# Bidirectional GLA encoder trunk: one rounded product per tile for the decay gate logits

## The chip, the cores and the metric

The kernel runs on one core of a Trainium2 chip. The metric is the device time of one execution in microseconds; a shorter one is better. The engines are PE (TensorE matrix products), DVE (VectorE), ACT (ScalarE), POOL (GpSimd) and SP, which here only issues transfers.

## The reference, cut to what matters

One encoder layer over 2560 tokens (512 and 2048) of width 1024. A projection of the normed input feeds gated linear attention (GLA) in both directions, differential attention and attention into a memory; they are gated, merged and projected. The change is about the decay gates of the GLA:

```python
glr = glr.astype(jnp.float32).reshape(B, T, 2, GLA_RANK)          # 2 x 16 columns of the projection
gate_logits = jnp.einsum('btir,irk->btik', glr, w2.astype(jnp.float32)) + b2.astype(jnp.float32)
log_a = jax.nn.log_sigmoid(gate_logits) / GLA_TAU
...
b = jnp.cumsum(ac, axis=2)                                        # per chunk, inside gla_scan
```

## The kernel before, in words

The kernel is a row of phases: projection (names `proj_`), forward GLA (`glaf_`), backward GLA (`glab_`), differential attention (`diff_`), cross attention (`cross_`) and merge (`merge_`). Each is a block with one hand-written instruction stream per engine; at its end all engines meet. A large product keeps the precision of fp32 by splitting both operands into a part rounded to fp32r and the rest, and adds three fp32r products (high x high, high x low, low x high).

**Projection.** Five chunks of 512 tokens, and the memory. In each chunk PE computes 8 "values" units, one "narrow" unit (the 32 gate columns) and 16 "stream" units of 24 products each. `product` gives the narrow unit 16 products: rows 0 to 31 of its bank take high x (high + low) and rows 32 to 63 take low x high, so the two halves are still to be added. ACT copies all 64 rows out of PSUM (`evacuate`, L393) and stores them to the scratch tensor `glrT`. DVE rounds the streamed weights (`split`, L476), one unit ahead where its order lets it, and POOL subtracts to get their low parts (L514); PE waits for that by `lo_split` before each stream unit.

**Forward GLA.** Twenty tiles of 128 tokens, all alike, each with 7 units of a second, independent product, `Dense` (168 fp32r products of 512 columns per tile), cut into slots between the GLA's own steps. Every unit of `Dense` needs a weight split: ACT rounds (L705), as soon as it has copied a finished unit out (L714), and POOL subtracts (L731, two inputs in SBUF). The tile's own chain is:

- PE: running sums of the log decays (L937), 60 dense products, `logits(j + 1)` (L920: one fp32 product of 65 rows, which the profile shows as two records), the plain scores (L951), 18 dense, level scores of the first group (L902, 56 records), 18 dense, level scores of the second group (L902, 48 records), and so on for the other direction, then outputs (L969 to L976) and 18 dense.
- ACT: exponents of the sums, then `softplus(j + 1)` on the new logits (L990 to L992), with the dense copies between.
- DVE: differences of the sums (L1091, L1092), four pairs of multiplications K and Q (`mix`, L1101 and L1103, two inputs in SBUF), between the third and the fourth pair the diagonal (L1128), after them `decays(j + 1)` (L1073, the rounding L1074, L1075), then the `copy_predicated` of the levels (L1139).

PE's second group of level scores may start when DVE has done the first four L1139 of the direction, since the four PSUM slots are used again:

```python
def levels(j, d, first, last):
    pe.wait_ge(picked_done, j * PK + 1 + d * NL + first)
```

The first tile is laid out a little differently in time, and the last one has no `logits` and no `decays`.

**Semaphores.** The two blocks made with `last=True` (differential attention and merge) end in a clearing of the semaphores used so far on POOL and one more barrier.

Of the kernel before, what the change touches and what calls it, by code (L numbers as in the profile page):

```python
# [12 lines left out]
P = 128  # L13
# [79 lines left out]
class Early:  # L93
# [113 lines left out]
def phase_project(nc, used, h, early, w_zg, w2, ident, x_all, gains, ident_dram, w_stream, w_narrow, w_values, w_mem, w_mem_values, hT_hi, hT_lo, featT, featT_lo, narrowT, values,  # L207
                  memkT, mem_v):

    with ExitStack() as ctx:  # L210
# [41 lines left out]
        stat = m.sb("stat", [P, 2, 4])  # L252
        acc = m.ps("acc", [P, BANKS, CH])
# [18 lines left out]
        low_stored = m.sems("low_stored", 2)  # L272
        stored = m.sems("stored", OUTS)
# [34 lines left out]
        @block.sync  # L308
        def _(sp):
            def load_x(n):  # L310
                if n >= 2:
                    sp.wait_ge(normed, n - 1)
                sp.dma_start(x[:, n % 2], rows(x_all, n * P, P)).then_inc(x_in[n % 2], 16)

            def load_piece(n):
                if n >= RAW:
                    sp.wait_ge(lo_split, n - RAW + 1)
                sp.dma_start(raw_of(n), source(n)).then_inc(raw_in[n % RAW], 16)

# [12 lines left out]
            for n in range(6, RESIDENT):  # L332
                load_piece(n)
            sp.dma_start(gain[:, 1], gains[:, 1]).then_inc(mem_gain_in, 16)
            for c in range(NC):
                for s in range(STREAM):
                    load_piece(RESIDENT + c * STREAM + s)
                    if s in (0, 1, 7, 8):
                        load_x((c + 1) * TT + (0, 1, 7, 8).index(s))
            for n in range(RESIDENT + NC * STREAM, len(pieces)):  # L340
                load_piece(n)
            sp.wait_ge(stored[narrow_units[0] % OUTS], 16 * (narrow_units[0] // OUTS + 1))
            early.load_gates(sp, narrowT, w2)
            sp.wait_ge(lo_split, len(pieces))
            early.load_w(sp, 0, w_zg, FORWARD_UNITS)

        @block.scalar
        def _(act):
# [32 lines left out]
            def evacuate(u):  # L381
                kind, c, i, t = units[u]
                act.wait_ge(unit_done, u + 1)
                if u >= OUTS:
                    act.wait_ge(stored[u % OUTS], 16 * (u // OUTS))
                    if in_parts(u - OUTS):
                        act.wait_ge(low_out, part_units.index(u - OUTS) + 1)
                if in_parts(u):
                    scale = HD ** -0.5 / SLOPES[i - DQ_BLOCK] if i < DK_BLOCK else 1.0
                    act.activation(out[:, u % OUTS].bitcast(FP32R), acc[:, u % BANKS], ACT.Copy, scale=scale).then_inc(evacuated, 1)  # L390
                else:
                    filled = slice(0, 2 * NR if kind == "narrow" else P)
# [12 lines left out]
                act.dma_start(dst, out[0:2 * NR if kind == "narrow" else P, u % OUTS]).then_inc(stored[u % OUTS], 16)  # L405
# [32 lines left out]
            for b in range(2):  # L438
                act.wait_ge(low_stored[b], 16 * (len(part_units) // 2))
            for b in range(OUTS):  # L440
                act.wait_ge(stored[b], 16 * ((len(units) + OUTS - 1 - b) // OUTS))

        @block.vector
        def _(dve):
# [41 lines left out]
            dve.memset(early.glr[4 * RANK:4 * RANK + 1, :, :], 1.0).then_inc(early.ones_ready, 1)  # L486
# [30 lines left out]
        def _(pe):  # L517
# [254 lines left out]
def phase_gla_forward(nc, used, h, early, ident, featT, narrowT, w2, v_dram, sums_dram, picked_dram, diag_dram,  # L772
                      o_dram, qb_dram, kb_dram, decb_dram, hT_hi, hT_lo, w_zg, zg):

    with ExitStack() as ctx:
# [8 lines left out]
        KR, N2 = 4 * RANK + 1, 2 * H * GK  # L784
# [6 lines left out]
        m.allocated += [*glr_in, decay_in, early.ones_ready]  # L791
# [68 lines left out]
        def _(sp):  # L860
# [33 lines left out]
        def _(pe):  # L894
# [28 lines left out]
            pe.wait_ge(decay_in, 16)  # L923
# [226 lines left out]
def phase_gla_backward(nc, used, h, early, ahead, ident, v_dram, o_dram, qb_dram, kb_dram, decb_dram, gain_dram, item_hi, item_lo, hT_hi, hT_lo, w_zg, zg):  # L1150

    with ExitStack() as ctx:
# [40 lines left out]
        block = m.block(used)  # L1193
# [190 lines left out]
def phase_diff(nc, used, ahead, front, ident, v_dram, lambda_dram, gain_dram, zg, item_hi, item_lo):  # L1384

    with ExitStack() as ctx:
# [72 lines left out]
        block = m.block(used, last=True)  # L1459
# [901 lines left out]
def build(nc, x_all, gains, w_stream, w_glr, w_values, w_mem, w_mem_values, w2, gla_sums, gla_picked, gla_diag,  # L2361
# [6 lines left out]
    featT, glrT = scratch("featT", N_FEAT, P, TOK), scratch("glrT", 4 * RANK, TOK)  # L2368
# [8 lines left out]
    with ExitStack() as ctx:  # L2377
# [3 lines left out]
        with ExitStack() as ahead_ctx:  # L2381
            with ExitStack() as gla_ctx:
# [3 lines left out]
                phase_project(nc, used, h, early, w_zg, w2, ident_tile, x_all, gains, ident, w_stream, w_glr, w_values, w_mem, w_mem_values, hT_hi, hT_lo,  # L2386
# [32 lines left out]
def layout(x_prompt, x_sample, mem_prompt, mem_sample, norm_g, w_in, gla_gate_w2, gla_gate_b, gla_norm_g,  # L2419
           diff_lambda, diff_norm_g, mem_norm_g, w_mem_kv, w_branch, w_out, final_norm_g):  # L2420
    w, at = w_in[0], OFFSETS
    w2 = np.zeros((4 * RANK + 1, 2, H * GK), w.dtype)
    for d in range(2):
        for part in range(2):
            w2[(2 * part + d) * RANK:(2 * part + d + 1) * RANK, d] = gla_gate_w2[0, d]
        w2[4 * RANK, d] = gla_gate_b[0, d]
# [12 lines left out]
        "w2": w2.reshape(4 * RANK + 1, -1),  # L2439
# [27 lines left out]
```

## Time and profile before

| | us |
|---|---|
| median of 3 runs | 3427.72 |
| lowest and highest run | 3424.59, 3429.3 |
| span of the profiled execution | 3421.6 |
| PE busy in the span | 3279.7 |
| forward GLA, PE from its first logits to the last level scores | 768.8 to 1746.4 |

The profiled execution is given by its span, from the first to the last instruction, 3421.6 us; the median of the timed runs is 6.1 us above it, which is what lies around the span. A row of a timeline has the start in us, the duration in us, engine, line, operation, output <- inputs, shape, how many instructions are merged, and in brackets how long the engine was idle before it and whose result ended that. A duration can hold time in which an issued instruction was still held up. Ends of PE rows are modelled, so what a PE instruction costs is read from start to start.

### The profile page before, as it was taken

To read this page: it belongs to the slowest core of one execution; us is meant where nothing else is said; L and a number is where in the kernel's file an instruction comes from. 1 tells how busy PE (TensorE), PEld (TensorE's weight loads), DVE (VectorE), ACT (ScalarE), POOL (GpSimd) and SP (SyncE) were. 2 spreads that over 40 slices of the span, in tenths; PEclk is the share of its full clock that TensorE was granted. 3 is DMA by queue.
4 is the path that set the end of the run, shared out by engine and by line. 5 is a ranking of instruction groups with operands and counts; after the bars stand their busy time and mean duration, and the time that the engine had idled before them with its cause. 6 is when DMAs were issued, how large, how long until landed. Compare 5 with 4: busy or idle time off the path is not lost. (4 is left out here: it accounts for less than half of the span.)

```text
span 3421.6 us, 51012 instructions
## 1 busy us (share of the span) xinstructions
PE 3279.7 (96%) x19032; PEld 2553.4 (75%) x19032; DVE 2014.6 (59%) x4689; ACT 1324.5 (39%) x2165; POOL 1223.2 (36%) x511
## 2 busy tenths in 40 slices
PE   7999999999999999999999988999999988999998
PEld 6888888877777777787777764666666556888887
DVE  3322312227556655665567788888888556556654
ACT  3111111114333433343333335666666555233332
POOL 3322313244333333333333326777777533000000
PEclk9999999999999999999999999999999999999999
DMA  6545445555454544544448964121221266666562
GB/s 213 182 156 184 167 153 167 179 200 182 137 176 136 184 146 129 183 145 137 130 160 288 324 215 139 59 75 55 73 65 38 99 218 234 222 234 231 181 216 77
DMA packets 317907, 554.90 MB, mean 162 GB/s; under 512 B 35421, under 2 KB 114525, under 8 KB 317662
## 3 DMA queue, kind: packets, MB, share of 16 engines
q1 hardware_dynamic: 266510, 471.26, 42.8%
q10 hardware_dynamic: 51152, 80.38, 6.5%
q8 instruction: 152, 2.49, 0.3%
q14 instruction: 93, 0.76, 0.1%
HBM read 382.03 MB, written 169.50 MB: 161 GB/s over the span
## 5 line engine op out<-in xcount | busy, mean ns | idle before, releaser
L731 POOL TENSOR_TENSOR glaf_w_lo<-early_raw,glaf_w_hi 128x1024 fp32r<-128x1024 f32 x140 | 350.7, 2506 | 650.3 <-ACT glaf_w_hi L705 650.3
L760 PE MATMUL glaf_dense_acc<-h_hi,glaf_w_hi 128*128 128x512 f32 x1120 | 452.7, 404 | 4.1 <-ACT glaf_dense_out L714 4.1
L760 PE MATMUL glaf_dense_acc<-h_lo,glaf_w_hi 128*128 128x512 f32 x1120 | 439.0, 392 | 0.0
L760 PE MATMUL glaf_dense_acc<-h_hi,glaf_w_lo 128*128 128x512 f32 x1120 | 436.8, 391 | 0.0
L1749 DVE CUSTOM_DVE_ANT_0 front_p<-diff_s_ps,ahead_table 128x512 f32<-128x512 f32 x544 | 346.7, 686 | 54.2 <-PE diff_s_ps L1611 53.0
L514 POOL TENSOR_TENSOR proj_w_lo<-early_raw,proj_w_hi 128x1024 fp32r<-128x1024 f32 x84 | 204.4, 2436 | 477.7 <-DVE proj_w_hi L476 477.7
L1572 POOL TENSOR_SCALAR front_p<-front_p,diff_ratio 128x1024 f32<-128x1024 f32 (+1 forms) x80 | 270.1, 3377 | 174.9 <-DVE diff_ratio L1769 174.9
L1692 ACT ACTIVATE front_p<-front_p,diff_neg_max 128x2048 f32<-128x2048 f32 (+1 forms) x160 | 278.9, 1744 | 10.1 <-DVE diff_neg_max L1759 10.0
L1635 PE MATMUL diff_oT_ps<-diff_aT,diff_v 128*128 128x512 f32 x544 | 273.8, 604 | 6.0 <-ACT diff_aT L1686 6.0
L201 PE MATMUL proj_acc<-h_hi,proj_w_hi 128*128 128x512 f32 x672 | 262.8, 391 | 0.0
L1610 PE MATMUL diff_s_ps<-ahead_k,ahead_q_high 128*128 128x512 f32 x544 | 245.1, 451 | 18.3 <-DVE diff_mx L1749 10.7
L203 PE MATMUL proj_acc<-h_hi,proj_w_lo 128*128 128x512 f32 x672 | 261.6, 389 | 0.0
L202 PE MATMUL proj_acc<-h_lo,proj_w_hi 128*128 128x512 f32 x672 | 261.5, 389 | 0.0
L760 PEld LDWEIGHTS glaf_dense_acc<-h_hi,glaf_w_hi 128*128 128x128 f32 x1120 | 211.8, 189 | 51.5 <-issue 7.9
L760 PEld LDWEIGHTS glaf_dense_acc<-h_hi,glaf_w_lo 128*128 128x128 f32 x1120 | 210.9, 188 | 45.6
L1139 DVE COPY_PREDICATED glaf_att<-glaf_picked,glaf_att_ps 128x256 f32<-128x256 int32 x280 | 146.7, 524 | 165.3 <-PE glaf_att_ps L902 158.4
L760 PEld LDWEIGHTS glaf_dense_acc<-h_lo,glaf_w_hi 128*128 128x128 f32 x1120 | 212.2, 189 | 40.6 <-issue 0.5
L1686 ACT ACTIVATE diff_aT<-diff_t_ps 128x512 f32<-128x512 f32 x272 | 159.4, 594 | 176.3 <-PE diff_t_ps L1624 176.2
L1624 PEld LDWEIGHTS diff_t_ps<-all_ident,diff_a 128*128 128x128 f32 x1088 | 133.9, 141 | 122.3 <-issue 95.4
L1611 PE MATMUL diff_s_ps<-ahead_k,ahead_q_low 128*128 128x512 f32 x544 | 217.2, 399 | 0.0
L393 ACT ACTIVATE proj_out<-proj_acc 128x512 f32<-128x512 f32 (+1 forms) x93 | 55.6, 598 | 412.0 <-PE proj_acc L203 394.5
L476 DVE CAST proj_w_hi<-early_raw 128x1024 fp32r<-128x1024 f32 x84 | 59.6, 715 | 251.8 <-PE proj_acc L203 251.8
(216 smaller groups left out, 7167.6 us busy)
## 6 DMA issues: line engine op xcount, KB each, us to landing
early_raw<-in_w_zg SPq DMA_DIRECT2D x180, 512.0 KB, 4.8
early_raw<-in_w_stream SPq DMA_DIRECT2D x80, 512.0 KB, 3.7
scratch_zg<-glaf_dense_out SPq DMA_DIRECT2D x140, 256.0 KB, 2.3
items_raw<-in_w_br SPq DMA_DIRECT2D x120, 256.0 KB, 2.9
merge_gate<-scratch_zg SPq DMA_DIRECT2D x120, 256.0 KB, 3.1
scratch_featT<-proj_out ACTq DMA_DIRECT2D x80, 256.0 KB, 2.3
items_br_hi<-scratch_item_hi SPq DMA_DIRECT2D x60, 256.0 KB, 5.9
items_br_lo<-scratch_item_lo SPq DMA_DIRECT2D x60, 256.0 KB, 6.4
```

What stands on the lines that cost most here:

```text
L201: pe.matmul(out, a_hi, b_hi, start=first, stop=False)
L202: pe.matmul(out, a_hi, b_lo, start=False, stop=False)
L203: return pe.matmul(out, a_lo, b_hi, start=False, stop=last)
L514: pool.tensor_tensor(lo, raw_of(n), hi, ALU.subtract).then_inc(lo_split, 1)
L731: pool.tensor_tensor(self.w_lo[:, s], self.raw[:, u % self.RAW], self.w_hi[:, s], ALU.subtract).then_inc(self.lo_split, 1)
L760: done = pe.matmul(self.acc[:, u % self.banks], a, x, start=i == 0, stop=i == self.PER - 1)
L1572: pool.tensor_scalar(p[:, o.slot, 1, half], p[:, o.slot, 1, half], ratio[:, o.slot:o.slot + 1], None, ALU.mult).then_inc(far_scaled, 1)
L1610: pe.matmul(s_ps[:, chunk % 2, i], q_high[:, b, i, cols], k[:, key % KS, i], start=True, stop=False)
L1611: done = pe.matmul(s_ps[:, chunk % 2, i], q_low[:, b, i, cols], k[:, key % KS, i], start=False, stop=True)
L1635: pe.matmul(oT_ps[:, :], v[:, o.head % 2, kt], aT[:, unit % 2], start=kt == 0, stop=kt == o.nk - 1).then_inc(values_done, 1)
L1692: act.activation(p[:, o.slot, i, 0:o.T], p[:, o.slot, i, 0:o.T], ACT.Exp, bias=neg_max[:, o.slot, i:i + 1], scale=SLOPES[o.h], accum_out=s ...
L1749: dve.tensor_tensor_reduce(out=p[:, n.slot, i, c * KC:(c + 1) * KC], in0=s_ps[:, (n.c0 + c) % 2, i], in1=table[:, start:start + KC], scale ...
```

## The change

The logits come from one fp32r product of 98 rows. For that the 32 gate rows are made whole in the projection (the two halves added) and split into a rounded and a low part: ACT copies rows 32 to 63, DVE adds them to rows 0 to 31 in PSUM, ACT rounds the sum out, DVE subtracts to get the low part. `glrT` now holds rounded, rounded again, low (96 rows), by three stores of 32 rows instead of one of 64, and two rows of ones stand below. The weight `decay_w` is split in the same manner by four DVE instructions (`split_decay`) ahead of chunk 1, from a load that SP issues early in the projection. Semaphores are cleared behind the backward GLA and no longer behind the differential attention.

```diff
-        self.glr = m.sb("glr", [4 * RANK + 1, 2, P])
-        self.decay_w = m.sb("decay_w", [4 * RANK + 1, 2 * H * GK])
+        self.glr = m.sb("glr", [GATE_ROWS, 2, P], FP32R)
+        self.decay_w = m.sb("decay_w", [GATE_ROWS, 2 * H * GK], FP32R)
...
+    def split_decay(self, dve, raw, pick):
+        whole = self.decay_w[:, :].bitcast(FP32)
+        step = Chain(dve, self.decay_steps)
+        dve.wait_ge(self.decay_in, 32)
+        step(dve.tensor_copy(self.decay_w[:, :], raw))
+        step(dve.tensor_tensor(raw, raw, whole, ALU.subtract))
+        step(dve.tensor_scalar(raw, raw, pick[:, 1:2], None, ALU.mult))
+        step(dve.scalar_tensor_tensor(self.decay_w[:, :], whole, pick[:, 0:1], raw, ALU.mult, ALU.add))
...
+            early.load_decay(sp, decay_raw[:, :], decay_pick[:, :], w2, w2_pick)
...
+                elif kind == "narrow":
+                    act.activation(out[0:NR, u % OUTS], acc[NR:2 * NR, u % BANKS], ACT.Copy).then_inc(gate_steps, 1)
+                    act.wait_ge(gate_steps, 3 * c + 2)
+                    act.activation(out[0:NR, u % OUTS].bitcast(FP32R), acc[0:NR, u % BANKS], ACT.Copy).then_inc(evacuated, 1)
...
                 if kind == "narrow":
-                    dst = narrowT[:, cols]
...
+                    act.dma_start(narrowT[0:NR, cols], out[0:NR, u % OUTS]).then_inc(gate_stored, 16)
+                    act.dma_start(narrowT[NR:2 * NR, cols], out[0:NR, u % OUTS]).then_inc(gate_stored, 16)
+                    act.wait_ge(gate_steps, 3 * c + 3)
+                    act.dma_start(narrowT[2 * NR:3 * NR, cols], out[NR:2 * NR, u % OUTS]).then_inc(stored[u % OUTS], 16)
+                    return
...
+            def gate_parts(u):
+                c, s = units[u][1], u % OUTS
+                near = acc[0:NR, u % BANKS]
+                dve.wait_ge(gate_steps, 3 * c + 1)
+                dve.tensor_tensor(near, near, out[0:NR, s], ALU.add).then_inc(gate_steps, 1)
+                dve.wait_ge(evacuated, u + 1)
+                dve.tensor_tensor(out[NR:2 * NR, s], near, out[0:NR, s], ALU.subtract).then_inc(gate_steps, 1)
...
             for u, (kind, c, i, t) in enumerate(units):
                 at = u - first_unit[c]
+                if u - 1 in narrow_units:
+                    gate_parts(u - 1)
+                if u == first_unit[1]:
+                    early.split_decay(dve, decay_raw[:, :], decay_pick[:, :])
                 for n in split_at.get(u, ()):
                     split(n)
...
+                    if u - BANKS in narrow_units:
+                        pe.wait_ge(gate_steps, 3 * units[u - BANKS][1] + 3)
...
-            pe.wait_ge(decay_in, 16)
+            pe.wait_ge(early.decay_steps, 4)
```

In each chunk the two new DVE instructions stand between two weight roundings. DVE before, in chunk 1 behind the narrow unit's start (L476 rounds the weights of stream units 0 and 1; `h_lo` belongs to the next chunk's norm):

```order
173 L458 SCALAR_TENSOR_TENSOR proj_xn<-proj_x,proj_stat,proj_gain 128x1024 [waits proj_transposed,proj_steps]
174 L476 CAST proj_w_hi<-early_raw 128x1024 [waits proj_unit_done,proj_raw_in1]
175 L476 CAST proj_w_hi<-early_raw 128x1024 [waits proj_unit_done,proj_raw_in2]
176 L465 TENSOR_TENSOR h_lo<-proj_tp,h_hi 128x4x128 [waits proj_hi_ready]
177 L465 TENSOR_TENSOR h_lo<-proj_tp,h_hi 128x4x128
```

The same place on DVE in the changed kernel:

```order
179 L487 SCALAR_TENSOR_TENSOR proj_xn<-proj_x,proj_stat,proj_gain 128x1024 [waits proj_transposed,proj_steps]
180 L505 CAST proj_w_hi<-early_raw 128x1024 [waits proj_unit_done,proj_raw_in1]
181 L519 TENSOR_TENSOR proj_acc<-proj_acc,proj_out 32x512 [waits proj_gate_steps]
182 L521 TENSOR_TENSOR proj_out<-proj_acc,proj_out 32x512 [waits proj_evacuated]
183 L505 CAST proj_w_hi<-early_raw 128x1024 [waits proj_unit_done,proj_raw_in2]
184 L494 TENSOR_TENSOR h_lo<-proj_tp,h_hi 128x4x128 [waits proj_hi_ready]
```

The rounding for stream unit 1 now stands behind two instructions that wait for the narrow unit and for ACT. In the forward GLA the order on every engine is as it was; PE there, in the changed kernel, with the logits as one product between the dense products and the plain scores:

```order
4035 L803 MATMUL glaf_dense_acc<-h_lo,glaf_w_hi 128x512
4036 L803 MATMUL glaf_dense_acc<-h_hi,glaf_w_lo 128x512
4037 L963 MATMUL glaf_z_ps<-early_decay_w,early_glr 128x512 [waits early_glr_in1,glaf_spans_ready,glaf_ends_ready]
4038 L994 MATMUL glaf_att_ps<-glaf_qk 64x64 [waits glaf_picked_done,glaf_qk_in0]
4039 L994 MATMUL glaf_att_ps<-glaf_qk 64x64 x7
```

The place and the waits are those of before (there L920); only the operands' type and rows differ.

## Rows read from the trace of the kernel before

**Rows 1.** The page's busy times over the whole span.

```profile
PE 3279.7 (96%) x19032; PEld 2553.4 (75%) x19032; DVE 2014.6 (59%) x4689; ACT 1324.5 (39%) x2165; POOL 1223.2 (36%) x511
```

**Rows 2.** The logits' line: records, ns min/median/max, first and last start.

```profile
L920 PE MATMUL glaf_z_ps<-early_decay_w,early_glr x40: 590/592/1192, 768.8 to 1675.9; 65*128 65x512 f32 x40
```

**Rows 3.** PE's timeline in tile 5 of the forward GLA.

```profile
1041.18 0.39 PE L760 MATMUL glaf_dense_acc<-h_hi,glaf_w_lo 128*128 128x512 f32 x1
1041.41 1.02 PE L920 MATMUL glaf_z_ps<-early_decay_w,early_glr 65*128 65x512 f32 x2
1042.36 0.46 PE L951 MATMUL glaf_att_ps<-glaf_qk 64*64 64x64 f32 x16
...
1047.08 1.12 PE L902 MATMUL glaf_att_ps<-glaf_Q,glaf_K 64*64 64x64 f32 x56
...
1053.24 0.90 PE L902 MATMUL glaf_att_ps<-glaf_Q,glaf_K 64*64 64x32 f32 x48 [0.73 <-DVE glaf_att L1139]
```

**Rows 4.** PE's waits: us in total, times, longest.

```profile
PE glaf_att_ps L902 <- DVE glaf_att L1139: 15.7, 20, 2.1
```

**Rows 5.** DVE's timeline in tile 5, and POOL's instruction beside it.

```profile
1046.95 1.21 DVE L1103 TENSOR_TENSOR glaf_Q<-glaf_X,glaf_qk 128x1024 f32<-128x1024 f32 x1
1048.09 0.68 DVE L1073 SCALAR_TENSOR_TENSOR glaf_L<-glaf_z_ps,glaf_log 128x512 f32<-128x512 f32 x1
1048.80 1.90 DVE L1074 CAST glaf_L_hi<-glaf_L 128x512 fp32r<-128x512 f32 x1
...
1051.35 1.84 DVE L1139 COPY_PREDICATED glaf_att<-glaf_picked,glaf_att_ps 128x256 f32<-128x256 int32 x4
...
1047.45 2.97 POOL L731 TENSOR_TENSOR glaf_w_lo<-early_raw,glaf_w_hi 128x1024 fp32r<-128x1024 f32 x1 [4.37 <-ACT glaf_w_hi L705]
```

**Rows 6.** An earlier Q of tile 5 and POOL's instruction beside it.

```profile
1035.15 3.43 DVE L1103 TENSOR_TENSOR glaf_Q<-glaf_X,glaf_qk 128x1024 f32<-128x1024 f32 x1
...
1035.07 2.43 POOL L731 TENSOR_TENSOR glaf_w_lo<-early_raw,glaf_w_hi 128x1024 fp32r<-128x1024 f32 x1 [2.72 <-ACT glaf_w_hi L705]
```

**Rows 7.** The last tile, without logits and decays: DVE and POOL.

```profile
1729.78 3.41 DVE L1103 TENSOR_TENSOR glaf_Q<-glaf_X,glaf_qk 128x1024 f32<-128x1024 f32 x1
1733.11 1.84 DVE L1139 COPY_PREDICATED glaf_att<-glaf_picked,glaf_att_ps 128x256 f32<-128x256 int32 x4
...
1729.37 2.73 POOL L731 TENSOR_TENSOR glaf_w_lo<-early_raw,glaf_w_hi 128x1024 fp32r<-128x1024 f32 x1 [3.48 <-ACT glaf_w_hi L705]
```

**Rows 8.** The first tile (tile 0): POOL, DVE and PE.

```profile
798.91 3.45 POOL L731 TENSOR_TENSOR glaf_w_lo<-early_raw,glaf_w_hi 128x1024 fp32r<-128x1024 f32 x1 [3.25 <-ACT glaf_w_hi L705]
...
798.93 1.21 DVE L1103 TENSOR_TENSOR glaf_Q<-glaf_X,glaf_qk 128x1024 f32<-128x1024 f32 x1
800.07 0.68 DVE L1128 TENSOR_TENSOR glaf_att<-glaf_att_ps,glaf_diag 128x512 f32<-128x512 f32 x1
...
804.50 0.68 DVE L1073 SCALAR_TENSOR_TENSOR glaf_L<-glaf_z_ps,glaf_log 128x512 f32<-128x512 f32 x1
...
806.28 1.86 DVE L1139 COPY_PREDICATED glaf_att<-glaf_picked,glaf_att_ps 128x256 f32<-128x256 int32 x4
...
800.89 1.12 PE L902 MATMUL glaf_att_ps<-glaf_Q,glaf_K 64*64 64x64 f32 x56 [2.29 <-DVE glaf_att L1128]
...
808.19 0.90 PE L902 MATMUL glaf_att_ps<-glaf_Q,glaf_K 64*64 64x32 f32 x48 [0.29 <-DVE glaf_att L1139]
```

**Rows 9.** PE in tile 4, whose weights come late behind a chunk's load.

```profile
1004.50 0.90 PE L902 MATMUL glaf_att_ps<-glaf_Q,glaf_K 64*64 64x32 f32 x48 [2.08 <-DVE glaf_att L1139]
```

**Rows 10.** The projection: the narrow unit's copy, and a weight split on POOL.

```profile
80.44 0.59 ACT L393 ACTIVATE proj_out<-proj_acc 64x512 f32<-64x512 f32 x1 [3.09 <-PE proj_acc L565]
...
87.55 2.39 POOL L514 TENSOR_TENSOR proj_w_lo<-early_raw,proj_w_hi 128x1024 fp32r<-128x1024 f32 x1 [17.53 <-DVE proj_w_hi L476]
```

**Rows 11.** PE's waits at the two phase ends: us in total, times, longest.

```profile
PE cross_s_ps L1922 <- PEq L74: 8.5, 1, 8.5
...
PE diff_s_ps L1610 <- PEq L1152: 7.4, 1, 7.4
```

More of the change, by code:

```diff
@@ L28 @@
 RANK = 16
+GATE_ROWS = 6 * RANK + 2
 TAU = 16.0
@@ L105, in __init__ @@
         self.decay_in = m.sem("decay_in")
+        self.decay_steps = m.sem("decay_steps")
         self.ones_ready = m.sem("ones_ready")
@@ L203, in product3, with phase_project @@
     return pe.matmul(out, a_lo, b_hi, start=False, stop=last)
-def phase_project(nc, used, h, early, w_zg, w2, ident, x_all, gains, ident_dram, w_stream, w_narrow, w_values, w_mem, w_mem_values, hT_hi, hT_lo, featT, featT_lo, narrowT, values,
+def phase_project(nc, used, h, early, w_zg, w2, w2_pick, ident, x_all, gains, ident_dram, w_stream, w_narrow, w_values, w_mem, w_mem_values, hT_hi, hT_lo, featT, featT_lo, narrowT, values,
                   memkT, mem_v):
@@ L341, in _ @@
                 load_piece(n)
+            sp.wait_ge(gate_stored, 32)
             sp.wait_ge(stored[narrow_units[0] % OUTS], 16 * (narrow_units[0] // OUTS + 1))
-            early.load_gates(sp, narrowT, w2)
+            early.load_gates(sp, narrowT)
             sp.wait_ge(lo_split, len(pieces))
@@ L390, in evacuate @@
                     act.activation(out[:, u % OUTS].bitcast(FP32R), acc[:, u % BANKS], ACT.Copy, scale=scale).then_inc(evacuated, 1)
-                else:
-                    filled = slice(0, 2 * NR if kind == "narrow" else P)
-                    act.activation(out[filled, u % OUTS], acc[filled, u % BANKS], ACT.Copy).then_inc(evacuated, 1)
+                elif kind == "narrow":
+                    act.activation(out[0:NR, u % OUTS], acc[NR:2 * NR, u % BANKS], ACT.Copy).then_inc(gate_steps, 1)
+                    act.wait_ge(gate_steps, 3 * c + 2)
+                    act.activation(out[0:NR, u % OUTS].bitcast(FP32R), acc[0:NR, u % BANKS], ACT.Copy).then_inc(evacuated, 1)
+                else:
+                    act.activation(out[:, u % OUTS], acc[:, u % BANKS], ACT.Copy).then_inc(evacuated, 1)
                 if u and in_parts(u - 1):
@@ L404, in evacuate @@
                     dst = memkT[i] if c == MEMC else featT[i, :, cols]
-                act.dma_start(dst, out[0:2 * NR if kind == "narrow" else P, u % OUTS]).then_inc(stored[u % OUTS], 16)
+                act.dma_start(dst, out[:, u % OUTS]).then_inc(stored[u % OUTS], 16)
             def high_resident(n):
@@ L790, in phase_gla_forward @@
         glr, decay_w, glr_in, decay_in = early.glr, early.decay_w, early.glr_in, early.decay_in
-        m.allocated += [*glr_in, decay_in, early.ones_ready]
+        m.allocated += [*glr_in, decay_in, early.decay_steps, early.ones_ready]
         log = m.sb("log", [P, N2])
@@ L1192, in phase_gla_backward @@
         stored = m.sems("stored", S)
-        block = m.block(used)
+        block = m.block(used, last=True)
         STEPS = 4 + RSQRT_STEPS
@@ L1458, in phase_diff @@
         stored = m.sems("stored", 2)
-        block = m.block(used, last=True)
+        block = m.block(used)
         NORM_STEPS = 2 + RSQRT_STEPS
@@ L2421, in layout @@
     w, at = w_in[0], OFFSETS
-    w2 = np.zeros((4 * RANK + 1, 2, H * GK), w.dtype)
+    w2 = np.zeros((GATE_ROWS, 2, H * GK), w.dtype)
     for d in range(2):
-        for part in range(2):
+        for part in range(3):
             w2[(2 * part + d) * RANK:(2 * part + d + 1) * RANK, d] = gla_gate_w2[0, d]
-        w2[4 * RANK, d] = gla_gate_b[0, d]
+        w2[6 * RANK:, d] = gla_gate_b[0, d]
+    high = np.repeat([1, 0, 1, 1, 0], [2 * RANK, 2 * RANK, 2 * RANK, 1, 1]).astype(np.float32)
     sums, picked = gla_matrices()
```

31 lines of the change are left out of this document (20 added, 11 removed).

## The prediction

> **What bounds the kernel now.** I read the busy times first: PE works 3279.7 of 3421.6 us [rows 1], so a shorter PE instruction looks like a shorter kernel. Then I asked in the list of PE's waits whether PE is ever the one that waits near the edited instruction. It is: PE waits for DVE's L1139 20 times, 15.7 us in all [rows 4], once in each tile of the forward GLA. In 15 of the 20 tiles (1 to 3, 5 to 7, 9 to 11 and 13 to 18) that wait is 0.73 us, as in tile 5 [rows 3]; tile 4 has 2.08 us [rows 9], tiles 0, 8, 12 and 19 have 0.29, 1.24, 0.58 and 0.57 us. So a tile is not PE's alone. From L937 to the second group of level scores it lasts as long as the DVE chain that L937 starts, and PE comes 0.73 us early. The logits stand on PE before this wait. What they save can only lengthen the wait, unless DVE's chain gets shorter too.
>
> **The logits.** Start to start, two neighbouring fp32r products of 512 columns are 1041.41 - 1041.18 = 0.23 us apart, and the fp32 product of the logits takes 1042.36 - 1041.41 = 0.95 us [rows 3]. The rows show no fp32r product of 98 rows. Its bounds are 0.23 us, as for 128 rows, and 0.59 us, one of the two records of now [rows 2]; I take 0.23, since the new product is the dense one with fewer rows. PE saves 0.72 us (bounds 0.36 and 0.72) in 19 tiles, 13.7 us.
>
> **Where it goes in a plain tile.** PE reaches the wait 0.72 us sooner. If DVE's chain ends when it ended, the whole saving becomes wait: 0.73 + 0.72 = 1.45 us, and the tile is as long as before.
>
> DVE's chain does not stay as it is. In it, POOL's weight subtraction and DVE's instructions with their sources in SBUF exclude each other. In [rows 6] POOL starts at 1035.07 for 2.43 us, and the Q that follows at 1035.15 takes 3.43 instead of 1.21 us. In [rows 5] it is the other way round for one instruction: POOL asks at 1047.45, while Q (1046.95, 1.21 us) has begun; POOL's record is 2.97 us, some 0.57 longer than its usual 2.4, and the rounding L1074, issued at 1048.80, ends only at 1050.70, just behind POOL (1050.42). The logic is that whoever is first keeps the other out for a whole instruction.
>
> POOL's instruction here belongs to the dense unit that ends 12 products behind the logits: PE ends the unit, ACT copies and rounds, POOL starts. ACT is idle before it, so this start moves with PE, from 1047.45 to 1046.73. The Q before which it must come starts at 1046.95, and K, ahead of it, occupies DVE until then. So POOL now asks 0.22 us before Q and is served when K ends. In [rows 6] an advance of 0.08 us was enough; in [rows 8] one of 0.02 us (798.91 against 798.93) was not. The order flips if the saving is over about 0.55 us.
>
> What the flip costs is to be seen in the last tile, which has no logits at all. There POOL asks at 1729.37, Q at 1729.78 takes 3.41 us, and the first L1139 starts at 1733.11, 3.33 us behind Q's start [rows 7]. A plain tile has `decays` between the two, 806.28 - 804.50 = 1.78 us where nothing holds it up [rows 8]. From Q's start to L1139 that is 3.33 + 1.78 = 5.11 us; before it was 1051.35 - 1046.95 = 4.40 us [rows 5]. DVE's chain gets 0.71 us longer, since Q, behind which everything stands, now waits for POOL, and not only the last two of `decays`. The tile gets 0.71 us longer and PE's wait grows to 0.73 + 0.72 + 0.71 = 2.16 us. Fifteen tiles: +10.7 us.
>
> The Trainium skill, page "SBUF — State Buffer", says that a DVE instruction with two SBUF inputs or in a two-port mode and a GpSimd instruction hold the shared port pair as an exclusive lock, for the whole instruction, whichever starts first. The trace agrees: 3.43 us in place of 1.21 [rows 6]. By that rule too an earlier POOL request is no gift.
>
> **Tiles 4, 8, 12 and 19.** In 4, 8 and 12 ACT waits for a weight that comes late from memory; DVE's end hangs on that, and PE's saving is absorbed: 0. Tile 19 has no logits: 0.
>
> **Tile 0 and the phase's start.** Here POOL asks at 798.91 and Q's start at 798.93 wins [rows 8]. At 0.72 us sooner POOL wins, and Q pushes L1128 from 800.07 to 798.93 + 3.33 = 802.26, 2.2 us, for which PE waits at 800.89. The later wait of 0.29 us goes. That is +1.9 us. The very first logits run on a cold PE, one record at 1.19 us [rows 2]; fp32r saves 1.4 us there, of which I count 1. Sum +1 us (bounds -1 and +3).
>
> **The clock.** A longer PE wait may cost more than itself. After the wait of 2.29 us in tile 0 the granted clock falls to 0.5 (1.2 GHz), and from 800.89 to 808.19 - 0.29 = 807.90 PE needs 7.01 us [rows 8]; the same work in tile 5 takes 1053.24 - 0.73 - 1047.08 = 5.43 us [rows 3]. So a fall costs 1.6 us. After 0.73 us nothing happens, and after 2.08 us in tile 4 the clock stayed at 1.0 (2.4 GHz) [rows 9]. The waits of 2.16 us stand between 2.08 and 2.29, in most of 18 tiles (tile 4 then at 2.8, tile 8 at 2.0). What PE does behind them is like behind the one that fell: some fifty tiny products (48 against 56 records) before dense work. I bound it by 0 and 18 falls and take 12: +19.2 us.
>
> **The projection.** ACT's copy of the narrow unit starts at 80.44 and takes 0.59 us [rows 10]. Now: copy 0.59, DVE's add 0.68 (as L1128, 512 columns from PSUM [rows 8]), copy 0.59, subtraction 0.68, then the rounding for stream unit 1 (0.7), then POOL 2.39 [rows 10], with five hand-overs of some 0.07: 6.0 us, to 86.4. Before, this rounding stood free. PE begins stream unit 0 when ACT's copy begins, or a little sooner, and has 24 products of 0.23 us for it, 5.5 us: it wants unit 1 at 85.9 or a little sooner. Stall 0.5 to 0.7 us in chunk 0. In chunks 1 to 4, PE has 8 transposes in between: 0 to 0.2 each. Behind the rounding on DVE stands the next chunk's norm, needed much later. The stores' two more issues on ACT, the bigger loads of `glr` (96 rows for 64), the early load of `decay_w` and the four `split_decay` instructions (under 3 us, while DVE sits idle through the values units) I count as 0; were that cover gone, they would cost 3 us once. Sum +1 us (bounds 0 and 4).
>
> **The clearing.** At the end of the differential attention PE waits 8.5 us with it, at the end of the backward GLA 7.4 us without [rows 11]. It moves from one exposed place to another: up to 1.1 us leave there and arrive here, sum 0.
>
> **Sum.** 10.7 + 1 + 19.2 + 1 + 0 = 31.9 us. The profiled span goes from 3421.6 to 3453.5 us, and with the 6.1 us around it the time from 3427.7 to 3459.6 us.
>
> **The rivals.**
> - *Collision, but the clock holds* (0.2). Waits of 2.16 us are harmless, as the 2.08 us were. 10.7 + 1 + 1 is about +13: 3440 us.
> - *All absorbed, no collision* (0.17). The new product is slower than 0.40 us or POOL's request comes too late to pass Q. Then 0.2 to 0.7 us a tile turn into wait and DVE's chain ends as now: 3427 to 3431 us. Against it speaks the last tile, where a request 0.41 us ahead passed.
> - *PE's saving counts* (0.08). This decides if DVE's chain shrinks with it: POOL would have to come so early that it is through before Q, or DVE's end is not what the second level scores wait for. Then 13.7 + 1 is saved and 2 are lost: 3415 us. The bracket on L902 names L1139 in every tile, so I give it little.
> - *Worse* (0.05): the clock falls in all 18 tiles and the projection loses 4 us: 3472 us and over.
>
> **How the numbers follow.** The forecast has 0.5; its own range is 3448 to 3470 (6 to 18 falls, tile 0 and projection within their bounds). For 8 in 10 I take 3428 to 3470, from the middle of the absorbed case to the top of the forecast. A measurement here tells 0.2% (6.9 us) from no change. Slower by more: 0.5 + 0.2 + 0.05, less a little, 0.74; within: 0.18; faster: 0.08.
>
> **What would show it.** After: in plain tiles the last Q at over 3.3 us and L1074 at under 1 us; POOL's fourth instruction of the tile at about 2.6 us and 0.7 us sooner; PE's wait <- L1139 at 2.1 to 2.2 us, 15 times, and a total over 35 us; a tile of 49.5 us where the clock holds and 51 where it falls; the granted clock below 1.0 in more of the forward GLA. Wrong would be a logits product at 0.4 us or more, a Q at 1.21, or a wait near 1.45 us.

## The result and the profile after

The changed kernel takes 3466.57 us (median of 4 runs, 3457.89 to 3469.89) against 3426.58 us (4 runs) on the same chip: a ratio of 1.011, 95% interval 1.0099 to 1.0122. The forecast was 3459.6 us, within 3428 to 3470. In the profiled executions the span goes from 3421.6 to 3456.1 us, +34.5 us.

The medians are 40.0 us apart, mainly since the profiled execution of the changed kernel is the shortest of its four: the other three have spans 7.2 to 12.0 us longer, at a mean granted clock of 0.976 to 0.978 instead of 0.979. By an estimate from these numbers (0.001 of 3460 us is 3.5 us of clock) most of that is more time at the lower clock; where it lay isn't shown. Timed runs lie 1.8 us above their spans (3457.89 against 3456.1), so of the 6.1 us that the prediction took for what lies around the span, the rest is that the profiled execution of the kernel before was a short one.

The page's busy times and the list of PE's waits (us in total, times, longest), to set beside [rows 1, 4, 11]:

```profile
PE 3293.8 (95%) x19012; PEld 2568.7 (74%) x19012; DVE 2030.7 (59%) x4703; ACT 1329.2 (38%) x2170; POOL 1213.1 (35%) x511
...
PE glaf_att_ps L945 <- DVE glaf_att L1182: 40.2, 20, 2.8
...
PE diff_s_ps L1653 <- PEq L75: 8.7, 1, 8.7
...
PE cross_s_ps L1965 <- PEq L1429: 7.0, 1, 7.0
```

PE has 20 records fewer, and is busy 14 us longer. Its wait before the second level scores grew from 15.7 to 40.2 us. Neither is what a saving of PE work looks like; a PE instruction at the lower clock counts as busy for longer.

The new product by its line, in the form of [rows 2]:

```profile
L963 PE MATMUL glaf_z_ps<-early_decay_w,early_glr x20: 391/391/628, 771.9 to 1711.8; 98*128 98x512 f32 x20
```

PE, then DVE, then POOL in tile 5, the tile of [rows 3, 5]. It begins at 1034.87, in the kernel before at 1026.83, so 8.04 us are to be taken off for a comparison:

```profile
1049.45 0.39 PE L963 MATMUL glaf_z_ps<-early_decay_w,early_glr 98*128 98x512 f32 x1
1049.77 0.46 PE L994 MATMUL glaf_att_ps<-glaf_qk 64*64 64x64 f32 x16
...
1062.01 1.21 PE L945 MATMUL glaf_att_ps<-glaf_Q,glaf_K 64*64 64x32 f32 x48 [2.08 <-DVE glaf_att L1182]
...
1055.02 3.40 DVE L1146 TENSOR_TENSOR glaf_Q<-glaf_X,glaf_qk 128x1024 f32<-128x1024 f32 x1
1058.34 0.68 DVE L1116 SCALAR_TENSOR_TENSOR glaf_L<-glaf_z_ps,glaf_log 128x512 f32<-128x512 f32 x1
1059.06 0.43 DVE L1117 CAST glaf_L_hi<-glaf_L 128x512 fp32r<-128x512 f32 x1
1060.13 0.91 DVE L1182 COPY_PREDICATED glaf_att<-glaf_picked,glaf_att_ps 128x256 f32<-128x256 int32 x2
...
1054.88 2.46 POOL L774 TENSOR_TENSOR glaf_w_lo<-early_raw,glaf_w_hi 128x1024 fp32r<-128x1024 f32 x1 [3.73 <-ACT glaf_w_hi L748]
```

Read from the bottom: POOL now asks 0.14 us before the last Q (1054.88 against 1055.02), where it asked 0.50 us behind it. The Q takes 3.40 instead of 1.21 us, the rounding behind it 0.43 instead of 1.90, and the first copy of L1182 starts 1060.13 - 1034.87 = 25.26 us into the tile instead of 1051.35 - 1026.83 = 24.52, 0.74 us later. PE came 0.63 us earlier (0.32 us from the logits to L994, before 0.95) and waits 2.08 us.

What follows this wait is not the same in every tile. Two stretches of PE's timeline in tiles 2 and 3, and PE's windows behind them (length, busy and count, granted clock, DMA share, GB/s):

```profile
910.45 0.90 PE L945 MATMUL glaf_att_ps<-glaf_Q,glaf_K 64*64 64x32 f32 x48 [2.06 <-DVE glaf_att L1182]
...
913.11 0.63 PE L803 MATMUL glaf_dense_acc<-h_hi,glaf_w_lo 128*128 128x512 f32 x1
913.53 0.63 PE L803 MATMUL glaf_dense_acc<-h_hi,glaf_w_hi 128*128 128x512 f32 x1
...
961.49 0.90 PE L945 MATMUL glaf_att_ps<-glaf_Q,glaf_K 64*64 64x32 f32 x48 [2.06 <-DVE glaf_att L1182]
...
964.22 0.39 PE L803 MATMUL glaf_dense_acc<-h_lo,glaf_w_hi 128*128 128x512 f32 x1
964.44 0.39 PE L803 MATMUL glaf_dense_acc<-h_hi,glaf_w_lo 128*128 128x512 f32 x1
```

```profile
912.24:915.65 3.41, 3.41 (x9) 0.50 0.74 219
...
963.50:967.50 4.00, 4.00 (x61) 1.00 0.75 234
```

The two waits are alike, 2.06 us. Behind the first, eight dense products run 0.43 us apart, at a granted clock of 0.5 (1.2 GHz); behind the second they run 0.23 us apart at 1.0 (2.4 GHz). So there are tiles of some 51.04 and of 49.45 us. Of tiles 1 to 18, sixteen lost the clock, and 3 and 17 did not. Tile 0 had the lower clock for 6.8 us in either kernel: before in two stretches (788.28 to 791.69 and 801.93 to 805.34), in the changed kernel in one (789.36 to 796.19).

The span's +34.5 us is this: the forward GLA from the start of tile 0 to that of tile 19 grew from 928.02 to 964.85 us, +36.8; ahead of it +1.8 (tile 0 starts at 783.38 instead of 781.61); behind it -4.1. The last two are mostly no effect of the change. In the ten executions profiled the stretch behind the start of tile 19 lasts 1708 to 1720 us: the lowest is the changed kernel's, the highest experiment 2's, which has all of the change too. And with the unchanged projection the narrow unit of chunk 0 began at 76.6 us in one profile and at 78.7 in another (experiment 5).

### The profile page after: what moved, and what is told of

Its sections match the earlier page's. It is cut to its first block and busy times, and to the rows that moved or that the text cites. A ratio compares the mean times of both kernels' runs of the same rounds, so it can differ in the third digit from the quotient of the medians.

```text
span 3456.1 us, 51000 instructions
## 1 busy us (share of the span) xinstructions
PE 3293.8 (95%) x19012; PEld 2568.7 (74%) x19012; DVE 2030.7 (59%) x4703; ACT 1329.2 (38%) x2170; POOL 1213.1 (35%) x511
## 5 line engine op out<-in xcount | busy, mean ns | idle before, releaser
L774 POOL TENSOR_TENSOR glaf_w_lo<-early_raw,glaf_w_hi 128x1024 fp32r<-128x1024 f32 x140 | 342.3, 2445 | 694.2 <-ACT glaf_w_hi L748 694.2
L803 PE MATMUL glaf_dense_acc<-h_hi,glaf_w_hi 128*128 128x512 f32 x1120 | 461.1, 412 | 4.5 <-ACT glaf_dense_out L757 4.1
L803 PE MATMUL glaf_dense_acc<-h_lo,glaf_w_hi 128*128 128x512 f32 x1120 | 447.5, 400 | 0.0
L803 PE MATMUL glaf_dense_acc<-h_hi,glaf_w_lo 128*128 128x512 f32 x1120 | 444.0, 397 | 0.0
L1182 DVE COPY_PREDICATED glaf_att<-glaf_picked,glaf_att_ps 128x256 f32<-128x256 int32 x280 | 146.2, 522 | 190.9 <-PE glaf_att_ps L945 184.1
L803 PEld LDWEIGHTS glaf_dense_acc<-h_hi,glaf_w_hi 128*128 128x128 f32 x1120 | 217.1, 194 | 54.0 <-issue 7.9
L803 PEld LDWEIGHTS glaf_dense_acc<-h_hi,glaf_w_lo 128*128 128x128 f32 x1120 | 215.9, 193 | 47.7
L803 PEld LDWEIGHTS glaf_dense_acc<-h_lo,glaf_w_hi 128*128 128x128 f32 x1120 | 217.3, 194 | 41.6
L417 ACT ACTIVATE proj_out<-proj_acc 128x512 f32<-128x512 f32 x88 | 52.7, 599 | 388.4 <-PE proj_acc L217 386.0
```

What stands on the lines that cost most here:

```text
L774: pool.tensor_tensor(self.w_lo[:, s], self.raw[:, u % self.RAW], self.w_hi[:, s], ALU.subtract).then_inc(self.lo_split, 1)
L803: done = pe.matmul(self.acc[:, u % self.banks], a, x, start=i == 0, stop=i == self.PER - 1)
```

## The experiments

All ratios are against the kernel before, on the same chip, with 95% intervals. Its medians were 3429.79 us for experiments 1 to 4, 3428.23 for the other four and 3426.58 for the changed kernel itself. Where times from different groups are set against each other below, some 3 us of the difference can come from that.

**1. The new product as fp32, all else changed.** It gives PE's 0.63 us back to the tile and leaves operands, projection and clearing as in the change.

```diff
-                pe.matmul(logits_bank(j), glr[:, j % S], decay_w[:, :], start=True, stop=True).then_inc(logits_ready, 1)
+                pe.matmul(logits_bank(j), glr[:, j % S].bitcast(FP32), decay_w[:, :].bitcast(FP32), start=True, stop=True).then_inc(logits_ready, 1)
```

> The changed kernel with one thing undone: the 98-row product of the logits is fp32 again (two records of 0.59 us), all the rest of the change stays. Collision theory (the cheaper product lets POOL's weight split pass the last Q on DVE, DVE's chain gets 0.7 us longer, PE's wait of 2.07 us makes the clock fall): L1146's last Q back at 1.21 us, PE's wait before the second level scores back at 0.73 us, plain tile back at 48.75 us, no falls; time 3430 us (3427 to 3434), the rest being what the projection and the phase start cost. Rival (the loss sits in the projection's gate work, the three stores or the bigger loads of the gate rows): the time stays near 3466 us, and wait and tile stay as in the changed kernel.

Measured: 3436.48 us, ratio 1.0019 (1.0007 to 1.0031), span 3432.2 us. Tile 5, which begins at 1029.96:

```profile
1050.09 1.21 DVE L1146 TENSOR_TENSOR glaf_Q<-glaf_X,glaf_qk 128x1024 f32<-128x1024 f32 x1
...
1051.93 1.90 DVE L1117 CAST glaf_L_hi<-glaf_L 128x512 fp32r<-128x512 f32 x1
...
1050.58 2.97 POOL L774 TENSOR_TENSOR glaf_w_lo<-early_raw,glaf_w_hi 128x1024 fp32r<-128x1024 f32 x1 [4.37 <-ACT glaf_w_hi L748]
...
1044.55 1.02 PE L963 MATMUL glaf_z_ps<-early_decay_w,early_glr 98*128 98x512 f32 x2
...
1056.38 0.84 PE L945 MATMUL glaf_att_ps<-glaf_Q,glaf_K 64*64 64x32 f32 x43 [0.73 <-DVE glaf_att L1182]
```

Row for row this is [rows 3, 5] again: POOL asks 0.49 us behind Q, the wait is 0.73, the tile 48.75 us. A slower product makes the kernel some 30 us faster. So most of the loss is in the time at which PE reaches what follows, and not in the projection, the loads or the clearing: the rest is 6.7 us. That is more than expected, and the time lies above the range of 3427 to 3434; what the profile shows of it stands at the end of the next section.

**2. The collision taken away on POOL's side.** In every tile that has a next one, POOL now waits until `decays` is through before it starts this weight subtraction, which is needed much later.

```diff
             for u in range(dense.count):
+                j, r = divmod(u - 5, 7)
+                if r == 0 and 0 <= j < N - 1:
+                    pool.wait_ge(L_steps, 3 * (j + 1) + 3)
                 dense.low(pool, u)
```

> The changed kernel in which POOL's one weight subtraction per tile that met the last Q waits until DVE has done the next tile's decays. Collision theory: last Q and the rounding of the logs both run unhindered (1.21 and 0.43 us), the first level copies start 23.0 us into the tile instead of 25.25, PE arrives at 25.1 us and no longer waits; tile 47.4 us (48.75 before, 51.05 in the changed kernel), no falls of the clock; time 3402 us (3396 to 3410). Rival (PE's wait has another cause than POOL, for instance DVE's own work or the loads): wait over 1 us stays and the time stays over 3440 us.

Measured: 3408.97 us, ratio 0.9946 (0.993 to 0.9962). Tile 5, from 1022.21:

```profile
1042.36 1.21 DVE L1149 TENSOR_TENSOR glaf_Q<-glaf_X,glaf_qk 128x1024 f32<-128x1024 f32 x1
...
1044.21 0.43 DVE L1120 CAST glaf_L_hi<-glaf_L 128x512 fp32r<-128x512 f32 x1
1045.28 1.88 DVE L1185 COPY_PREDICATED glaf_att<-glaf_picked,glaf_att_ps 128x256 f32<-128x256 int32 x4
...
1045.44 2.39 POOL L774 TENSOR_TENSOR glaf_w_lo<-early_raw,glaf_w_hi 128x1024 fp32r<-128x1024 f32 x1 [6.95 <-DVE glaf_L_lo L1121]
...
1047.22 0.90 PE L948 MATMUL glaf_att_ps<-glaf_Q,glaf_K 64*64 64x32 f32 x48
```

Neither Q nor the rounding is stretched, the copies start at 23.07 instead of 25.26 us, and PE's row has no bracket: the wait is gone, and a plain tile lasts 47.32 us. The three tiles with late weights (4, 8 and 12) keep waits of 2.4, 3.0 and 2.4 us and last 51.39, 52.01 and 49.77 us, together 5.2 us longer than before. That is most of the 7 us by which the time came above the 3402 expected; the plain tiles did as expected. This also shows what the collision cost in the kernel before, where it hit the rounding instead: 24.52 - 23.07 = 1.45 us of DVE's chain.

**3. The wait filled.** The collision stays; PE issues eight dense products more ahead of its wait, whose result the next unit overwrites. They are work that the kernel doesn't need.

```diff
                     dense.products(pe, slot + X_SLOTS + 1 + 2 * d)
+                    if d == 0 and j + 1 < N:
+                        dense.filler(pe, 8)
                     levels(j, d, LG, NL)
...
+    def filler(self, pe, n):
...
+        for k in range(n):
+            pe.matmul(self.acc[:, u % self.banks], self.w_hi[:, s, k % KT], self.h_hi[:, b, k % KT], start=True, stop=True)
```

> The changed kernel in which PE repeats 8 dense products (1.8 us, results overwritten) right before it waits for the second group of level scores. DVE's chain is untouched. Clock theory: the wait shrinks from 2.07 to about 0.25 us and the granted clock no longer falls, so every plain tile takes 49.46 us; 16 falls of 1.6 us are gone, time 3440 us (3434 to 3446). Rival (the tiles of 51 us are long for another reason than the clock): tiles stay at 51 us and the time at 3457 to 3470 us.

Measured: 3441.27 us, ratio 1.0041 (1.0025 to 1.0057). In tile 5, from 1035.86:

```profile
1056.00 3.40 DVE L1157 TENSOR_TENSOR glaf_Q<-glaf_X,glaf_qk 128x1024 f32<-128x1024 f32 x1
...
1060.76 1.97 PE L786 MATMUL glaf_dense_acc<-h_hi,glaf_w_hi 128*128 128x512 f32 x8
1063.01 0.90 PE L954 MATMUL glaf_att_ps<-glaf_Q,glaf_K 64*64 64x32 f32 x48 [0.28 <-DVE glaf_att L1193]
```

Q is still at 3.40 us and the chain as long as in the changed kernel, but the wait is 0.28 us and every plain tile lasts 49.48 us: no fall of the clock in any. With useless work of 1.8 us a tile the kernel is 25 us faster than without it. In the 13 plain tiles that had a fall this is the price of the clock alone, 51.04 - 49.48 = 1.56 us each, 20 us. The rest of the total is not: in the profiles tiles 4, 8 and 12 are 4.7 us shorter together, since their waits are filled too, and tile 0 is 4.7 us longer (53.55 us, see the next section). Between experiment 1 (48.75) and this one (49.48) lies the price of the collision alone, 0.73 us a tile.

**4. The wait filled with work that is needed.** The dense products come in fixed shares per slot of the tile. The slot ahead of the wait gets 27 instead of 18, the later ones fewer.

```diff
-        SHARES = [10] * X_SLOTS + [18] * 6
+        SHARES = [10] * X_SLOTS + [18, 27, 16, 16, 16, 15]
```

> The changed kernel with the same 168 dense products per tile shared out otherwise: 27 instead of 18 in the slot before the wait, 16, 16, 16, 15 instead of 18 in the four behind. The collision on DVE stays (last Q 3.4 us, first level copies at 25.25 us). Theory that the wait is idle time between a DVE chain and a PE that comes too soon: the nine products fill it, wait under 0.3 us, no falls, tile 47.4 us, time 3402 us (3396 to 3412). Rival (moved products only meet other waits: the other direction's level scores, ACT's copies): new waits on L945 or L803 of over 1 us per tile, time over 3430 us.

Measured: 3399.55 us, ratio 0.9921 (0.9903 to 0.9938), faster than both kernels. Tile 5, from 1020.39:

```profile
1040.53 3.40 DVE L1146 TENSOR_TENSOR glaf_Q<-glaf_X,glaf_qk 128x1024 f32<-128x1024 f32 x1
...
1045.64 1.86 DVE L1182 COPY_PREDICATED glaf_att<-glaf_picked,glaf_att_ps 128x256 f32<-128x256 int32 x4
...
1047.11 0.39 PE L803 MATMUL glaf_dense_acc<-h_hi,glaf_w_lo 128*128 128x512 f32 x1
1047.56 0.90 PE L945 MATMUL glaf_att_ps<-glaf_Q,glaf_K 64*64 64x32 f32 x48
```

The collision is there (3.40), and it costs next to nothing: DVE's copies end at 1047.50, about when PE gets there. The plain tile is 47.45 us. No wait on L945 or L803 over 0.42 us is left in tiles 1 to 18, so the rival's new waits did not come.

**5. The same shares in the kernel before.** The line of experiment 4, and nothing of the change.

> The kernel before, with only the new shares of dense products (27 in the slot ahead of the wait, 16, 16, 16, 15 behind). Theory that PE's wait in a plain tile is filled by any work that does not feed DVE: wait gone, plain tile 48.75 - 0.73 = 48.0 to 48.1 us, tiles 4, 8 and 12 alike; time 3414 us (3408 to 3419). Set against the changed kernel with the same shares (3399.6 us) it gives what the cheaper product is worth once the wait is filled: 19 x 0.61 = 11.6 us less 1 us in the projection. Rival (the gain of the shares in the changed kernel comes from the cheaper product alone): time stays at 3428 to 3432 us.

Measured: 3410.92 us, ratio 0.9951 (0.9932 to 0.9969); a plain tile is 47.93 us, without a wait. Now the change is worth 47.93 - 47.45 = 0.48 us a tile. In all it is 9.1 us by the profiled spans (3405.5 and 3396.4) and 3410.92 - 3399.55 = 11.4 us by the medians, which come from two groups. The rival in which PE's saving counts was not wrong about the product, only about this kernel: it needs a tile that PE bounds. Why it is 0.48 and not PE's 0.63 us, the next experiment shows.

**6. Shares and POOL's wait together.** The edits of 2 and 4 in the changed kernel.

> The changed kernel with both remedies, the new shares and POOL behind the decays. PE works through in each tile already with the shares alone (47.45 us), so removing the collision on DVE as well should bring next to nothing in plain tiles (47.3 to 47.4 us): 3398 us (3393 to 3404). If DVE's chain still cost PE something behind the shares, it would be under 3393 us.

Measured: 3399.4 us, ratio 0.9913 (0.9898 to 0.9929), the same as experiment 4 alone. In tile 5, from 1019.80:

```profile
1042.86 1.86 DVE L1185 COPY_PREDICATED glaf_att<-glaf_picked,glaf_att_ps 128x256 f32<-128x256 int32 x4
...
1046.53 0.39 PE L803 MATMUL glaf_dense_acc<-h_hi,glaf_w_lo 128*128 128x512 f32 x1
1046.84 0.90 PE L948 MATMUL glaf_att_ps<-glaf_Q,glaf_K 64*64 64x32 f32 x48
```

Here DVE is through 2.1 us ahead of PE, and the level scores start 0.31 us behind the last dense product; in experiment 4 it was 0.45. So with the shares alone PE still waited 0.13 us for DVE, too little for the view to put it in brackets, and the plain tile is 47.32 instead of 47.45 us. That is 2 us in 15 tiles. Longer waits in tiles 4, 8 and 12 (0.20, 0.76 and 0.65 us) take part of it back, and the medians don't show it. Once PE nearly bounds the tile, removing the collision buys next to nothing.

**7. Each new product twice.** The second overwrites the first with the same values, so PE does 0.23 us of useless work in each tile. POOL's request comes that much later (20.22 us into the tile instead of 20.01).

```diff
+                pe.matmul(logits_bank(j), glr[:, j % S], decay_w[:, :], start=True, stop=True)
                 pe.matmul(logits_bank(j), glr[:, j % S], decay_w[:, :], start=True, stop=True).then_inc(logits_ready, 1)
```

> The changed kernel that issues each logits product twice (the second overwrites the first). PE then saves 0.61 - 0.23 = 0.38 us per tile over the kernel before. Threshold theory (the loss hangs on POOL asking before the last Q starts, 20.12 us into the tile): POOL asks at 20.24, Q wins and takes 1.21 us, the rounding of the logs takes 1.9, level copies start at 24.52, wait 1.1 us, plain tile 48.75 us and no falls: 3436 us (3429 to 3442), 30 us faster than the changed kernel for 0.23 us MORE work per tile. Rival (the loss grows smoothly with what PE saves, or has to do with the rows and type of the product): tile at about 50 us, time near 3455 us or over.

Measured: 3434.75 us, ratio 1.002 (1.001 to 1.003). Tile 5, from 1030.23:

```profile
1045.04 0.40 PE L964 MATMUL glaf_z_ps<-early_decay_w,early_glr 98*128 98x512 f32 x1
...
1050.37 1.21 DVE L1147 TENSOR_TENSOR glaf_Q<-glaf_X,glaf_qk 128x1024 f32<-128x1024 f32 x1
...
1050.45 3.40 POOL L774 TENSOR_TENSOR glaf_w_lo<-early_raw,glaf_w_hi 128x1024 fp32r<-128x1024 f32 x1 [3.95 <-ACT glaf_w_hi L748]
...
1056.66 0.55 PE L945 MATMUL glaf_att_ps<-glaf_Q,glaf_K 64*64 64x32 f32 x24 [1.16 <-DVE glaf_att L1183]
```

POOL asks 0.08 us behind Q instead of 0.14 ahead of it. Q keeps its 1.21 us, POOL takes 3.40, the wait is 1.16 us and the plain tile 48.76 us, with no fall in any of the 15. One more matmul a tile, 0.23 us of it, makes the kernel some 30 us faster. The new product keeps its type and rows here, so these are not the cause. The loss has a threshold between a saving of 0.4 and one of 0.6 us a tile, and the change lies just beyond it.

**8. The clearing alone.** `last=True` moves from the differential attention to the backward GLA in the kernel before.

```diff
-        block = m.block(used)
+        block = m.block(used, last=True)
...
-        block = m.block(used, last=True)
+        block = m.block(used)
```

> The kernel before with only the clearing of semaphores moved from behind the differential attention to behind the backward GLA. Forecast: PE's wait at the first place grows by 1.1 to 1.3 us, at the second it shrinks by 1.5, the time is the same (ratio 0.999 to 1.001). Rival (the clearing costs more where transfers ahead of the next phase are under way): over 3 us slower.

Measured: 3429.94 us (12 runs), ratio 1.0003 (0.9994 to 1.0013): no difference. Its two waits:

```profile
PE diff_s_ps L1610 <- PEq L74: 8.7, 1, 8.7
...
PE cross_s_ps L1922 <- PEq L1386: 7.0, 1, 7.0
```

Together 15.7 us, before 8.5 + 7.4 = 15.9 [rows 11].

## Why the prediction was right, step by step

- **"What they save can only lengthen the wait."** Right. In the kernel before no part of the logits' saving could shorten a tile, and experiment 5 shows the one condition under which it does.
- **"PE saves 0.72 us."** Mis-sized: 0.63 us by the starts, and POOL's request moved by 0.61 (from 20.62 to 20.01 us into the tile). The new product is like the dense one (0.39 us), but the small products behind it start 0.32 us later, not 0.23. With 0.55 us as the step's own turning point, the forecast had less room than it seemed. That the flip came all the same is in part luck.
- **The collision, +0.71 us a tile.** Right. The chain's copies were forecast 0.71 us later and came 0.74 later; experiments 1 and 3 price it at 0.73. Experiment 2 shows the mechanism, since only POOL was moved there. The Trainium skill, page "SBUF — State Buffer", section "Who interferes with whom", says that the order of issue, not the shape of an operation, decides which of DVE and GpSimd is blocked. The trace agrees: the same pair of instructions gave Q 3.40 and POOL 2.46 us with POOL 0.14 us ahead, and Q 1.21 and POOL 3.40 us with POOL 0.08 us behind. What the records call the start is not quite the order of issue: with POOL 0.02 us ahead, Q still won [rows 8].
- **"PE's wait grows to 2.16 us."** 2.06 to 2.08 us: the collision as forecast, the saving 0.1 less.
- **The clock, 12 falls of 1.6 us, +19.2.** The mechanism and the price of one were right (51.04 - 49.45 = 1.59 us), the count mis-sized: 16 falls, +25.4 us. It is the term that decides the size of the loss, and experiment 3 shows it apart from the collision. The rival "the clock holds" put the time at 3440 us; experiment 3, where it held, measured 3441.27.
- **Tiles 4, 8 and 12, counted as 0.** Besides their falls, which are among the sixteen, they moved by -0.6, +0.9 and +0.6 us.
- **Tile 0, +1.9 us.** This step failed: the tile lasted 48.88 us, before 48.90. The prediction moved POOL's request by the saving and left the clock where it had fallen before. In the changed kernel the logits of tile 0 take 0.63 us, as at 1.2 GHz, and start 12.28 us into it instead of 11.28; the clock was low ahead of them. POOL's request came 0.62 us later than before, not 0.72 sooner, and didn't pass Q. The wait behind was 1.66 instead of 2.29 us, the clock held there, and what PE had gained went into the second wait, 1.84 instead of 0.29 us. This is not the product's doing: experiment 1, with the fp32 product, has the same single stretch of lower clock in tile 0. In experiment 3 the clock fell as in the kernel before, and there the predicted chain is to be seen in tile 0, which begins at 784.62:

```profile
801.35 2.89 POOL L774 TENSOR_TENSOR glaf_w_lo<-early_raw,glaf_w_hi 128x1024 fp32r<-128x1024 f32 x1 [2.66 <-ACT glaf_w_hi L748]
...
801.97 3.36 DVE L1157 TENSOR_TENSOR glaf_Q<-glaf_X,glaf_qk 128x1024 f32<-128x1024 f32 x1
...
806.07 1.92 PE L954 MATMUL glaf_att_ps<-glaf_Q,glaf_K 64*64 64x64 f32 x56 [5.02 <-DVE glaf_att L1182]
```

  POOL asks 0.62 us ahead of Q, Q is stretched, and PE waits 5.02 us. That tile lasted 53.55 us. So the mechanism of the step holds, and its premise, the place of the clock's fall, does not.
- **The phase's start, -1 us.** Not shown. From the first logits to tile 0 it is 11.50 us in the changed kernel and 12.79 in the kernel before, but 11.74 and 11.75 in experiments 5 and 8, which have the same logits as the kernel before. So 0.2 us is what can be seen of it.
- **The projection, a stall of 0.5 to 0.7 us in chunk 0, +1 in all.** Right. The chain and its end, from ACT's copy to PE's wait:

```profile
82.60 0.59 ACT L413 ACTIVATE proj_out<-proj_acc 32x512 f32<-32x512 f32 x1 [3.09 <-PE proj_acc L608]
83.22 0.69 DVE L519 TENSOR_TENSOR proj_acc<-proj_acc,proj_out 32x512 f32<-32x512 f32 x1 [16.29 <-ACT proj_out L413]
83.94 0.59 ACT L415 ACTIVATE proj_out<-proj_acc 32x512 fp32r<-32x512 f32 x1 [0.75 <-DVE proj_acc L519]
84.56 0.68 DVE L521 TENSOR_TENSOR proj_out<-proj_acc,proj_out 32x512 f32<-32x512 f32 x1 [0.66 <-ACT proj_out L415]
85.27 0.69 DVE L505 CAST proj_w_hi<-early_raw 128x1024 fp32r<-128x1024 f32 x1
...
88.58 0.47 PE L215 MATMUL proj_acc<-h_hi,proj_w_hi 128*128 128x512 f32 x1 [0.56 <-POOL proj_w_lo L555]
```

  From the narrow unit of chunk 0 to that of chunk 4 the projection takes 552.5 us, before 551.6. All six experiments with the changed projection have 552.4 to 552.6, both with the old one 551.6.
- **The clearing, 0.** Right, by experiment 8.
- **The sum.** In the profile 15 x 0.70 + 16 x 1.59 + 0.9 = 36.8 us for tiles 1 to 18 (0.70 = 49.45 - 48.75), as measured; 10.7 + 1 + 19.2 = 30.9 us had been forecast for all tiles and the phase's start. In the profile the total, 34.5 us against 31.9, came near because the 6.2 us of falls too few are mostly offset by tile 0 and by the 4.1 us behind the start of tile 19, which the prediction did not have. That is luck. By the medians, 40.0 us, the forecast is 8 us too low.

What stays open: experiment 1 is 6.7 us above the kernel before (2.4 to 10.6 by its interval), of which the projection's 0.9 us is located. Its profile has another 4.1 us between tiles 0 and 19: 0.0 in every plain tile, and 1.7 and 2.1 in tiles 4 and 8, whose late weights let PE wait 2.22 and 1.80 us, with a fall behind each. Experiment 8's profile shows the same in tile 8 (wait 2.25 us, tile 51.80) without a line of the gates' change, so it varies between executions, and whether the change makes it more frequent was not tested. Why tiles 3 and 17 of the changed kernel kept the clock behind the same wait wasn't found either.

## What to carry to other kernels

Before a shorter instruction is booked as a gain, find the wait that follows it on its engine: if there is one, the saving lands there, and what matters is who is triggered earlier. Where two engines exclude each other, note for each pair by how many tenths of a microsecond they miss one another now; an edit that is smaller than this margin is harmless and one beyond it is not (here, at a margin of some 0.55 us, a saving of 0.40 us in experiment 7 and one of 0.61 us in the change). Where a wait on PE is long enough to be followed by the lower clock, move needed work into it: here nine dense products in another slot turned a loss of 1.1% into a gain of 0.8%. Of that gain the move alone brings 0.5% (experiment 5), and the cheaper product the rest.

## What was not expected of the hardware

- The order between POOL and DVE flips within 0.22 us: asked 0.14 us ahead, POOL stretched Q from 1.21 to 3.40 us in all 15 plain tiles; asked 0.08 us behind, in none. All ten profiles together narrow it to 0.04 us: in the 418 cases in which POOL's record begins 0.07 to 0.49 us ahead of a K or Q of the forward GLA, that one takes 3.38 to 3.44 us; in the two with 0.02 and 0.03 us (tile 0 of the kernel before and of experiment 8) it takes 1.21.
- In the changed kernel a wait of 2.06 to 2.11 us was followed by a granted clock of 0.5 in 14 of 16 tiles that had it (1 to 7, 9 to 11 and 13 to 18), in experiment 7 one of 1.16 us in none of 15, and one of 2.08 us in tile 4 of the kernel before in none either [rows 9]. The tile's own useful work was the same. Over all profiles the length of the wait alone doesn't tell: waits of 1.80 (experiment 1, tile 8), 1.84 (changed kernel, tile 12) and 2.10 us (experiment 7, tile 8) were followed by the lower clock, waits of 1.77 (experiment 7, tile 12), 2.26 (experiment 8, tile 4) and 2.38 us (experiment 2, tile 12) were not.
- A fall can begin later than the wait: in tile 2 the first dense products behind it still run at 2.4 GHz, 0.23 us apart, and only those from 912.25 on at 1.2 GHz; in tile 5 the small products behind it take 1.21 us instead of 0.90. Both lose 1.6 us.
